# Mixer A (gated delta rule): query Gram and states in other PSUM bank pairs, attention and second values at other levels, finer hooks and half splits in the output product

## What is computed

```python
kb = k * beta[..., None]
L = jnp.where(strict, jnp.einsum("bhnid,bhnjd->bhnij", kb, k) * decay, 0.0)
...
sol = lax.linalg.triangular_solve(L, rhs, left_side=True, lower=True,
                                  transpose_a=False, conjugate_a=False, unit_diagonal=True)
u, w = sol[..., :DV], sol[..., DV:]
a_qk = jnp.einsum("bhnid,bhnjd->bhnij", q, k) * decay
...
def step(S, inp):
    qd, kd, u_c, w_c, a_c, gl = inp
    v_new = u_c - jnp.einsum("bhck,bhkv->bhcv", w_c, S)
    o = jnp.einsum("bhck,bhkv->bhcv", qd, S) + jnp.einsum("bhij,bhjv->bhiv", a_c, v_new)
    S = S * gl[..., None, None] + jnp.einsum("bhck,bhcv->bhkv", kd, v_new)
    return S, o
...
o = rmsnorm(o, out_norm) * jax.nn.silu(zf)
return o.reshape(Bsz, T, HV).astype(h.dtype) @ w_out
```

## Time and profile before

| what | value |
|---|---|
| median of 3 runs | 1675.61 us (1666.07 to 1679.09) |
| profiled execution | 1671.28 us |
| its span, first to last instruction | 1669.5 us |
| TensorE busy | 1582.7 us, 95% |
| VectorE busy | 1068.3 us, 64% |
| ScalarE busy | 725.0 us, 43% |
| mean granted TensorE clock | 0.976 of full |

### The profile page before, as it was taken

One profiled execution on the slowest core, in us unless ns is written; L12 is line 12 of the kernel. 1 busy time (PEld: TensorE's weight loads), 2 busy tenths in 40 slices (PEclk: granted clock), 3 DMA queues, 4 the chain that ended last, 5 costly groups with the idle time before them and its releaser, 6 DMA issues.

```text
span 1669.5 us, 35598 instructions
## 1 busy us (share of the span) xinstructions
PE 1582.7 (95%) x15413; PEld 1521.2 (91%) x15413; DVE 1068.3 (64%) x1269; ACT 725.0 (43%) x806; POOL 78.0 (5%) x53
## 2 busy tenths in 40 slices
PE   7999999878899999999998999999968999999998
PEld 7999899777899999999988999998957778999997
DVE  6775587653766547664577766477676654877446
ACT  5443445432534335333456434364633333465333
POOL 2000000000100001000101000021020000100000
PEclk9999999988999999999999999999989998999999
DMA  8665545101556555655534565554300011555562
GB/s 270 195 194 190 172 154 175 52 2 47 156 177 189 189 180 180 195 177 194 176 111 125 180 199 194 186 188 133 127 1 2 3 52 33 183 190 197 185 198 76
DMA packets 155063, 243.23 MB, mean 146 GB/s; under 512 B 9283, under 2 KB 106174, under 8 KB 154814
## 3 DMA queue, kind: packets, MB, share of 16 engines
q1 hardware_dynamic: 154510, 240.63, 44.5%
q10 hardware_dynamic: 432, 0.79, 0.2%
HBM read 240.34 MB, written 1.05 MB: 145 GB/s over the span
## 4 chain that ended last, share of the span: by engine, by line
PE 86%; DVE 7%; ACT 4%; issue 2%; DMA 1%; POOL 0%; SPq 0%; ACTq 0%; DVEq 0%
PE dense_ps L2376 24%; PE dense_ps L2377 23%; PE dense_ps L2378 23%; PE mixer_ps L449 3%; PE dense_ps L449 2%; DVE w_lo L2746 1%; PE mixer_ps L1646 1%; PE mixer_ps L1086 1%; ACT ly_r L495 0%; PE mixer_ps L1077 0%; DVE xT L2864 0%; DMA raw<-in_ffn_w_gu 0%; ACT score_b L1116 0%; ACT w_hi L2573 0%; PE mixer_ps L1652 0%
## 5 line engine op out<-in xcount | busy, mean ns | idle before, releaser
L2376 PE MATMUL dense_ps<-h_hi,w_hi 128*128 128x256 f32 x2368 | 666.8, 282 | 11.8 <-DVE h_lo L2821 8.2
L2746 DVE TENSOR_TENSOR w_lo<-raw,w_hi 128x2048 fp32r<-128x2048 f32 x225 | 523.1, 2336 | 241.7 <-ACT w_hi L2573 240.8
L2377 PE MATMUL dense_ps<-h_lo,w_hi 128*128 128x256 f32 x2368 | 660.8, 279 | 0.0
L2378 PE MATMUL dense_ps<-h_hi,w_lo 128*128 128x256 f32 x2368 | 660.7, 279 | 0.0
L2573 ACT ACTIVATE w_hi<-raw 128x2048 fp32r<-128x2048 f32 x225 | 428.5, 1913 | 332.4 <-DMA raw<-in_ffn_w_down 117.8
L2376 PEld LDWEIGHTS dense_ps<-h_hi,w_hi 128*128 128x128 f32 x2368 | 448.2, 189 | 18.2 <-issue 17.7
L2378 PEld LDWEIGHTS dense_ps<-h_hi,w_lo 128*128 128x128 f32 x2368 | 447.7, 189 | 0.0
L2377 PEld LDWEIGHTS dense_ps<-h_lo,w_hi 128*128 128x128 f32 x2368 | 446.8, 189 | 0.8 <-issue 0.5
L2376 PE MATMUL dense_ps<-g_hi,w_hi 128*128 128x256 f32 x960 | 266.7, 278 | 0.0
L2377 PE MATMUL dense_ps<-g_lo,w_hi 128*128 128x256 f32 x960 | 266.7, 278 | 0.0
L2378 PE MATMUL dense_ps<-g_hi,w_lo 128*128 128x256 f32 x960 | 266.7, 278 | 0.0
(11 more groups left out here) (532 smaller groups left out, 1839.2 us busy)
## 6 DMA issues: line engine op xcount, KB each, us to landing
raw<-in_ffn_w_gu SPq DMA_DIRECT2D x176, 512.0 KB, 4.7
raw<-in_ffn_w_down SPq DMA_DIRECT2D x88, 512.0 KB, 4.1
raw<-in_w_ff SPq DMA_DIRECT2D x64, 512.0 KB, 4.3
raw<-in_w_in SPq DMA_DIRECT2D x36, 512.0 KB, 4.4
raw<-in_a_w_in SPq DMA_DIRECT2D x32, 512.0 KB, 4.1
raw<-in_a_w_out SPq DMA_DIRECT2D x8, 512.0 KB, 4.1
raw<-in_b_w_in SPq DMA_DIRECT2D x8, 512.0 KB, 4.3
raw<-in_b_w_out SPq DMA_DIRECT2D x8, 512.0 KB, 4.1
```

What stands on the lines that cost most here:

```text
L2376: pe.matmul(o, hi, mh, start=start, stop=False)
L2377: pe.matmul(o, hi, ml, start=False, stop=False)
L2378: return pe.matmul(o, lo, mh, start=False, stop=stop)
L2746: dve.tensor_tensor(w_lo[:, p % SLOTS, :], raw[:, p % SLOTS, :], w_hi[:, p % SLOTS, :].bitcast(F32), ALU.subtract).then_inc(lo_ready, 1)
```

## The change

Sizes and numbers are as before. On PE the query Gram goes to banks 2 and 3 of `mixer_ps`. For group 0 it waits for `a_dsub` and `a_erow` (which level 1's hook waited for), and for group 1 for `a_vn0`. The wait for `a_att` moves from level 0 to level 2 in both inverses, the square sums of group 1's keys from level 1 to 2, and the wait for `k_dec` of group 1 from level 2 to 3. `keys_turned(1)` and `states(0)` change tensor and change places. On ACT `decays(1)` moves behind the last level. On DVE `attention` moves from level 0 to 1, `key_decay(1)` from 2 to 0, `second_values(0)` from 3 to 2, `key_norm(1)` from 3 to 5, and `splits(1)` from level 5 to behind `second_values(1)`. In the output product the three hooks stand after 12, 24 and 36 matmuls, and `finished` works in two halves of two heads each. `values_kept(0)` is written elsewhere but stays where it was on DVE.

```diff
@@ PE
-            to = banks(0 if with_q else 2, 2, D_ps)
+            to = banks(2, 2, M_ps if with_q else D_ps)
...
         gram(0, False)
+        pe.wait_ge(a_dsub, 1)
+        pe.wait_ge(a_erow, 1)
         gram(0, True)
 
         def beside_first(lv):
             if lv == 0:
                 keys_turned(0, banks(2, 1, D_ps))
+            if lv == 2:
                 pe.wait_ge(a_att, 1)
-            if lv == 1:
-                pe.wait_ge(a_dsub, 1)
-                pe.wait_ge(a_erow, 1)
                 pe.wait_ge(a_sq, 3)
                 square_sums(1, 0, M_ps[:, 2:4, :])
-            if lv == 2:
                 pe.wait_ge(a_kdec, 1)
...
         def beside_second(lv):
             if lv == 0:
+                keys_turned(1, banks(2, 1, D_ps))
+                states(0, banks(3, 1, D_ps))
+            if lv == 1:
+                state_keys(0, banks(3, 1, D_ps))
+            if lv == 2:
                 pe.wait_ge(a_att, 2)
-                states(0, banks(3, 1))
-                keys_turned(1, banks(2, 1))
-            if lv == 1:
-                state_keys(0, banks(3, 1))
-            if lv == 2:
-                pe.wait_ge(a_kdec, 2)
                 second_values(0, banks(2, 1))
             if lv == 3:
+                pe.wait_ge(a_kdec, 2)
                 outputs(0, banks(2, 2, D_ps))
...
         gram(1, False)
+        pe.wait_ge(a_vn0, 1)
         gram(1, True)
...
-        wide("a_out", o_hi, o_lo, (a_osplit, lambda r: r + 1), beside_output)
+        wide("a_out", o_hi, o_lo, (a_osplit, lambda r: max(r + 1, 2)), quarter=beside_output)
@@ ACT, beside_first
-            if lv == 1:
+            if lv == 2:
                 logs(1, 0)
-            if lv == 2:
-                roots(1, 0)
             if lv == 3:
                 logs(1, 1)
+                roots(1, 0)
             if lv == 4:
                 roots(1, 1)
-            if lv == 5:
-                decays(1)
             if lv == 6:
                 row_decays(1)
+                decays(1)
@@ DVE, finished
-            o_ = tiles(2, g)
...
+            for e in range(2):
+                o_ = tiles(2, g)[:, 2 * e:2 * e + 2, :]
+                k2 = slice(4 * g + 2 * e, 4 * g + 2 * e + 2)
+                link(dve.tensor_tensor(o_, banks(2 + e, 1, (D_ps, M_ps)[g]).rearrange("p (h b) i -> p h (b i)", b=2),
+                                       sq[:, 4 + 2 * e:6 + 2 * e, :], ALU.mult))
+                link(dve.scalar_tensor_tensor(out=o_, in0=o_, scalar=column("a_out_norm"), in1=z_gate[:, k2, :],
+                                              op0=ALU.mult, op1=ALU.mult))
+                split_act(o_, o_hi[:, k2, :], o_lo[:, k2, :]).then_inc(a_osplit, 1)
@@ DVE, beside_first, beside_second and after
-            if lv == 3:
-                key_norm(1)
...
             if lv == 5:
                 decay_less(1, range(4, 8))
+                key_norm(1)
...
-            if lv == 5:
-                splits(1)
...
         second_values(1)
+        splits(1)
         finished(1)
         splits(2)
```

More of the change, by code:

```diff
@@ L704, in mixer_a_pe, with beside_output @@
         state_keys(1, banks(0, 1))
-        def beside_output(k):
-            if k == 0:
+        def beside_output(at_):
+            if at_ == 0:
                 second_values(1, banks(1, 1))
-            if k == 1:
+            if at_ == 1:
                 pe.wait_ge(a_oln, 1)
                 outputs(1, banks(2, 2))
-            if k == 2:
+            if at_ == 2:
                 output_sums(1, M_ps[:, 0:2, :])
-        wide("a_out", o_hi, o_lo, (a_osplit, lambda r: r + 1), beside_output)
+        wide("a_out", o_hi, o_lo, (a_osplit, lambda r: max(r + 1, 2)), quarter=beside_output)
     def mixer_a_act(act, link, narrow, splits):
@@ L786, in state_kept @@
             act.wait_ge(a_s, g + 1)
-            act.activation(state[:, :, :], banks((3, 1)[g], 1), ACT.Copy).then_inc(a_state, 1)
+            act.activation(state[:, :, :], banks((3, 1)[g], 1, (D_ps, M_ps)[g]), ACT.Copy).then_inc(a_state, 1)
         def output_square(g):
@@ L943, in attention @@
             dve.wait_ge(a_kq, g + 1)
-            dve.tensor_tensor(SET_A[g]["att_t"][:, :, :], banks(0, 2, D_ps), dec_t[:, :, :], ALU.mult).then_inc(a_att, 1)
+            dve.tensor_tensor(SET_A[g]["att_t"][:, :, :], banks(2, 2), dec_t[:, :, :], ALU.mult).then_inc(a_att, 1)
             dve.wait_ge(a_erow, g + 1)
@@ L951, in key_decay @@
             dve.wait_ge(a_gate[6], 1)
-            dve.tensor_tensor(SET_A[g]["k_dec"][:, :, :], banks(2, 1, (D_ps, M_ps)[g]),
+            dve.tensor_tensor(SET_A[g]["k_dec"][:, :, :], banks(2, 1, D_ps),
                               over_free(gate(K_DECAY)[:, 4 * g:4 * g + 4, 0], P), ALU.mult).then_inc(a_kdec, 1)
@@ L962, in remaining @@
             for h in range(HG):
-                last = dve.scalar_tensor_tensor(out=rest[:, h, :], in0=banks((3, 0)[g], 1)[:, h, :],
+                last = dve.scalar_tensor_tensor(out=rest[:, h, :], in0=banks((3, 0)[g], 1, (D_ps, M_ps)[g])[:, h, :],
                                                 scalar=of_gate(NEG_EG, g, 2 * h + 1),
@@ L974, in finished @@
             dve.wait_ge(a_ors, g + 1)
-            o_ = tiles(2, g)
-            link(dve.tensor_tensor(o_, banks(2, 2, (D_ps, M_ps)[g]).rearrange("p (h b) i -> p h (b i)", b=2), sq[:, 4:8, :],
-                                   ALU.mult))
             dve.wait_ge(a_z, 1)
[L979 to L982, removed]
+            for e in range(2):
[6 more added lines that the diff above has]
+                split_act(o_, o_hi[:, k2, :], o_lo[:, k2, :]).then_inc(a_osplit, 1)
         for c in range(6):
@@ L1003, in mixer_a_dve @@
         narrow("a_in", beside_gates, 0, 6, 1, False)
-        narrow("a_in", lambda _c, _q: None, 0, 7, 1, True)
-        values_kept(0)
+        narrow("a_in", lambda _c, _q: values_kept(0), 0, 7, 1, True)
         lower(0)
         def beside_first(lv):
-            if lv == 0:
-                attention(0)
             if lv == 1:
                 key_decay(0)
+                attention(0)
+            if lv == 2:
                 gate_upto(1)
-            if lv == 3:
-                key_norm(1)
             if lv == 4:
@@ L1019, in beside_first @@
                 decay_less(1, range(4, 8))
+                key_norm(1)
             if lv == 6:
-                query_norm(1)
                 dve.wait_ge(piece_used, PIECE_OF["a_out"])
                 values_kept(1)
+                query_norm(1)
         def beside_second(lv):
             if lv == 0:
-                attention(1)
+                key_decay(1)
             if lv == 1:
                 remaining(0)
+                attention(1)
             if lv == 2:
-                key_decay(1)
-            if lv == 3:
                 second_values(0)
-            if lv == 5:
-                splits(1)
         def inverse(g, beside):
```

## The result

The changed kernel took 1651.22 us (median of 4 runs, 1643.35 to 1659.54) against 1673.70 for the kernel before (4 runs, 1666.07 to 1679.09): 0.9874 of its time, 95% interval 0.9826 to 0.9921. A second measurement gave 0.9866 (0.981 to 0.9922); one of its eleven runs of the kernel before, at 2611.18 us with a granted clock of 0.556, is left out of that. Forecast were 1650 and a gain of 23.2 us; the medians of the first measurement differ by 22.5, those of the second by 18.8.

The account below looks back on a forecast made before the run. PE was taken as the bound, ending last for 86% of the span, losing time to waits and half clock. Eight terms in mixer A summed to -23.2 us, 1671.28 to 1648.1, forecast as 1650; range 1641 to 1661.

Parts of the forecast that it names:

- 1 attention off level 1, group 0: First inverse: query Gram in other banks, so PE starts level 1 without waiting for attention; -3.3 us, -2.1 with clock down.
- 2 last level, with key norm's +0.4: First inverse's last level: exponential behind ly_a removes PE's stop, -2.8 us; key norm before the copies costs +0.4.
- 3 values, Grams, level 0: First values, both Grams and level 0 run partly at full clock; ends -3.2 and -1.3, middle taken, -2.2 us.
- 4 states without attention: Second inverse: group 0's states use another bank and no longer wait for attention, 17.0 us become 10.6; -6.4 us.
- 5 v_new at level 2: Second inverse: v_new made at level 2 instead of 3, so PE's 1.57 us idle goes; -1.6 us.
- 6 split moved: Second inverse's last level: w_lo split leaves the front of DVE's copies for behind the last v_new; -0.6 us.
- 7 to the product's start: Before the output product: finished() in two halves takes 5.2 us instead of 4.5 on DVE; +0.4 us.
- 8 output product: Output product: earlier hooks and halves of finished() ready before PE wants them, no stop, full clock; -7.1 us.
- A: Rival: PE's clock falls in mixer A's new stretches, costing 5 us, 1653 to 1655; chance 0.17.
- D: Slower rival: 64x64 passes at first inverse's levels 1 and 2 leave the clock at half, 1677 us; chance 0.04.
- C: Rival: output product's last a_out piece loads late, losing 4 us, 1654; chance 0.05.
- B: Rival: DVE becomes the bound, with attention, remaining and key norm before a level's copies; 7 us, 1657; chance 0.10.

Follow-up runs that it names:

- x3: Changed kernel with group 0's attention back at level 0 on DVE and PE's wait for it before level 1; mixer A stretch 108.43 us against 102.64.
- x4: Changed kernel with group 1's attention and PE's wait for it back at level 0 of the second inverse; mixer A stretch 109.50 us against 102.64.
- x5: Changed kernel with ACT's exponential of dec_t for group 1 back in front of the last level's ly_a; mixer A stretch 105.07 us against 102.64.
- x9: Changed kernel with group 1's k_dec back at level 2 and second_values(0) at 3, PE's k_dec wait at 2; mixer A stretch 107.18 us against 102.64.
- x1: Changed kernel with hooks back after 24, 48 and 72 matmuls and finished() whole; mixer A stretch 106.83 us against 102.64.
- x2: Changed kernel with finished() whole and the finer hooks kept; mixer A stretch 103.35 us against 102.64.
- x8: Changed kernel with group 0's finished() whole and spread over DVE's idle times; mixer A stretch 103.49 us against 102.64.
- x10: x8 with group 1's key norm at level 4 on DVE; 1656.19 us over five rounds, changed kernel 1658.66; mixer A stretch 102.94 us.
- x6: Changed kernel with the w_lo split back at level 5, before the second inverse's last copies on DVE; mixer A stretch 104.07 us against 102.64.

## Why the prediction was right

PE's walk, measured from the first Gram, before and now, as differences by term, for both profiles of the changed kernel:

| term | forecast | first profile | second |
|---|---|---|---|
| 1 attention off level 1, group 0 | -3.3 | -3.6 | -3.6 |
| 2 last level, with key norm's +0.4 | -2.4 | -2.4 | -2.4 |
| 3 values, Grams, level 0 | -2.2 | -3.2 | -0.7 |
| 4 states without attention | -6.4 | -6.5 | -6.5 |
| 5 v_new at level 2 | -1.6 | -1.6 | -1.6 |
| 6 split moved | -0.6 | -0.5 | -0.5 |
| 7 to the product's start | +0.4 | +0.2 | +0.2 |
| 8 output product | -7.1 | -7.5 | -5.9 |
| sum | -23.2 | -25.1 | -21.0 |

Each is the start of one row less that of the same row before, both from their first Gram: term 1 is (328.54 - 311.24) - (326.53 - 305.59). The product's start before is the 399.52 of the earlier trace rows; PE's timeline has its first row at 399.29, by which term 7 is +0.5 and term 8 -7.7.

- *Terms 1, 2, 4, 5:* right by mechanism and size, and x3, x4, x5 and x9 bring the idles back. In the same walk each of these experiments takes longer in the terms that its edit touches (x3 3.45 us in term 1, x4 5.8 in 4, x5 1.56 in 2, x9 1.9 in 4 and 1.6 in 5), and all others but 3 and 8 stay as they were, within 0.1 us. Terms 3 and 8 hold the clock's changes from profile to profile.
- *Term 3:* between the bounds -3.2 and -1.3 it took the middle. The first profile gave the full-clock end, the second -0.7, outside the bounds. Of the eleven profiles with the new order nine had the clock down at the first L592 or the Grams, and eight of them give -1.8 or -1.9. The bound -1.3 was wrong in its working too: it let DVE's neg_lt end last, but PE runs from L592 through level 0 without an idle in both profiles, and what sets the time is how long half clock lasts. That the term is near the average of the two is luck.
- *Term 7:* the sum was right by luck, for its working was not. The forecast took 0.7 us of longer finished() against 0.4 of slack at an unchanged half clock (0.3 by these numbers, where the sum has 0.4). At full clock states and state_keys end 2.2 us before DVE is through with finished(0). What was won there on PE (1.8 us) was lost to a new wait on DVE, and half clock followed for 3.4 us. The price of the halves stood: the product starts 7.15 us behind L592 with them and 6.5 without (x1, x2). So did the fixed cost of small tiles: 0.68 against 1.23 for half the elements, so the row's 0.15 and not the 0.06 from the table of the Trainium skill ("VectorE: DVE Perf Modes", TRN2 errata).
- *Term 8:* the step on the hooks held (sums start at T + 9.4, forecast 9.5), and x1 against x2 shows its worth: a stop of 4.20 us or of 0.22. The step on the halves had them ready 2 us early, which was true and of no use: x2 shows that a whole finished() costs 0.22 us there, and in front of the product halves cost 0.64.
- *Rivals:* A, the clock falling in the new stretches, is part of every profile (1.7 and 5.8 us lost in the changed kernel), at the Grams, the states and the product's start. It came at level 1 only in x3, which has the stop there again. The second profile is such a case. D did not come: levels 1 and 2 of the first inverse, all 64x64, ran at a clock of 1.00 in both profiles of the changed kernel and in every experiment but x3. C did not either. B did not come as it was told, but DVE is the bound in front of the output product, where no rival looked. The last levels are the other place where DVE ends last, by 1.15 and 0.71 us.
- *Between runs:* the forecast put the whole spread into its range as noise. The traces show a cause for much of it, below. With four runs over 16 us, a median within 1.2 us of the forecast is partly luck. The chance of 0.83 for faster by over 1% is below what its own parts add up to (0.64, most of 0.17 and 0.05, half of 0.10: about 0.9).

## What to carry to other kernels

Read a stage by two sums, engine idle and busy time at half clock: idle gave 13.0 us of the gain in both profiles, half clock 13.0 in one and 8.9 in the other. A single wait has no fixed price in clock: x3 and x4, with waits of 2.13 and 3.50 us, lost about 3 us more than the other experiments, while x5 and x9, with 2.25 us and with 1.84 and 1.57, lost no more than those. When a wait in front of an engine goes, ask which chain of another engine was hidden by the slow stretch that goes with it: the next limit was a row of VectorE work in front of the output product. Compare small changes by the stretch that they touch, and within it from row to row, where profiles agree to 0.1 us as long as the clock does; the rest of a 1650 us program moves by more than they do.

## What the runs showed of the hardware

Dense matmul stages run at one of two rates with the clock at 1.00 in both. The table by stretch of the kernel before, two stretches of PE busy throughout:

```profile
100.00:120.00 20.00, 20.00 (x179) 20.00 (x178) 13.43 (x15) 8.62 (x6) 0.00 (x0) 1.00 0.63 196
540.00:560.00 20.00, 20.00 (x172) 20.00 (x171) 13.75 (x13) 8.71 (x6) 0.00 (x0) 1.00 0.60 204
```

and of the changed kernel:

```profile
100.00:120.00 20.00, 20.00 (x173) 20.00 (x172) 12.93 (x11) 6.90 (x5) 0.00 (x0) 1.00 0.60 196
700.00:720.00 20.00, 20.00 (x179) 20.00 (x178) 14.08 (x14) 8.12 (x6) 0.00 (x0) 1.00 0.64 211
```

179 matmuls in 20 us against 172, 4% apart, for the same code, or a matmul every 0.113 us against every 0.118; the same stage is fast in one profile and slow in another. A rate often holds for a whole stage (429 to 617 us in the changed kernel's first profile is slow throughout) and mostly changes where PE's steps show a hesitation of 0.2 to 0.3 us. I count as slow each 10 us stretch outside mixer A's with a mean step over 0.116 us and at most one step over 0.13. A line fitted to the twelve profiles gives everything outside mixer A's stretch as 1527 us + 0.041 of the slow time, and single profiles lie up to 4 us off it; the slope is what 0.113 against 0.118 gives. Slow time runs from 60 us (x1) over 410 (before) to 700 (changed) and 740 (x8). The difference of 290 us between the profiled pair is worth 12 us by that slope, near the 13.1 by which the changed kernel was slower outside the stretch. So the profiled pair differs by less than the medians, and runs without a trace may spread for the same reason.

What picks the rate was not tried. Slow time was least in x1 to x4 (60 to 220 us), which ran on another chip than x5 to x10 and the second profile (380 to 740). The kernel before took 1656.00 us beside the first four and 1684.50 beside x5, x6, x8 and x9, so the chip or the hour may have a part in it, and the totals of x1 (1637.33) and x2 (1634.03) can't be set against those of the others. For the changed kernel's first profile, to hold the fast rate everywhere would be worth about 29 us (an estimate, 700 times 0.041), more than this change.
